# The gated unit's groups on three banks in turn, and a job of 16 columns as four column strips

## The chip, the cores and the metric

The kernel runs on one core of one Trainium2 chip. A core has five engines with queues of their own: TensorE (PE in the profile; its weight loads are listed apart as PEld), VectorE (DVE), ScalarE (ACT), GpSimd (POOL) and SyncE (SP, which here only issues DMAs). They meet through semaphores. TensorE writes into PSUM, which the kernel holds as one tensor `P` of 128 partitions by 8 banks by 512 float32; ScalarE and VectorE read it from there. The metric is the device time of one execution in microseconds (us), the median of several runs.

## What is computed

One step of a decoder block: two branches from one input projection, merged by gates, then a mixture of experts. The part that matters here, cut from the reference:

```python
h = _rmsnorm(x, norm_mix_w)
proj = h @ w_in                       # 1024 -> 4624 columns
qkv, z, a, b, u, gate_a, gate_b = jnp.split(proj, cuts, axis=-1)
...
g = -jnp.exp(a_log) * jax.nn.softplus(a + dt_bias)      # 8 columns "a": the decay of each head
beta = jax.nn.sigmoid(b)                                # 8 columns "b": the gate of each head
o, s_new = _gated_delta(q, k, v, g, beta, s_delta)
...
ys = jax.nn.gelu(ys).astype(x.dtype)                    # branch two, 512 channels
ys = ys * jax.nn.sigmoid(ys @ w_glu)                    # the gated unit
y_b = ys @ w_b_up
```

There are 1024 prompt tokens and 32 sample tokens, 1056 in all, and everything is float32.

## The kernel before

The activations `hT` lie transposed in SBUF: 8 slabs of 128 channels by 1056 tokens. The input projection runs as 32 **jobs** (36 with those that come later), each of which makes 128 columns of `proj` for all tokens: for each of the 8 slabs, three matmuls of 352 tokens (`NBK = 3`, `TBK = 352`), one for each of three PSUM banks. Even jobs write banks 0 to 2, odd jobs banks 3 to 5 (line 688). Job n waits until its weights are in (`s_w`, a ring of three) and until job n-2 has been read out of PSUM (`s_jev`, which counts jobs that were read). A float32 matmul of the program is two pairs of a weight load and a matmul in the trace, so a job of 24 matmuls has 48 records on TensorE.

The order on each engine is the order in which its block is written. Around the change it is this:

- **Jobs 8 to 15** make gate columns. ScalarE reads each out with a sigmoid and stores it to `gate_d`.
- **The gated unit** (lines 846 to 854) comes after job 15: for each of 4 blocks of 128 output channels, three groups over the tokens (408, 408 and 272 columns), each of 4 matmuls that add up in one bank. Every group takes bank 7 through `bank7()`, which waits until the group before has been read. ScalarE reads a group with a sigmoid (line 2140); after each third, VectorE multiplies (lines 1516 and 1518), and ScalarE stores the product to `y2_d` (lines 2144 and 2146). After the fourth it waits until the stores have landed and raises `s_free` (line 2149), since what comes next lies in the same SBUF.
- **Job 16**, called `AB`, has only 16 useful columns, the 8 of `a` and the 8 of `b`. Its weights are loaded by two DMAs to columns 0 to 7 and 32 to 39 of a block of 64 (line 2462), and its matmuls are 64 columns wide. The results are in partitions 0 to 7 and 32 to 39 of three banks. ScalarE reads them with two activations (line 2155): one adds `dt_bias` on the way, the other is the sigmoid of `beta`. Both go into the tile `G0`.
- **The decay chain** follows: VectorE (line 1527) and ScalarE (lines 2162 to 2164) make the softplus with two more tables of functions, VectorE ends it with a running sum (lines 1529 to 1532), and SyncE sends it out (line 2539 on).
- **Job 17 on** make q, k and v. ScalarE reads job 17 (lines 2215 to 2226), VectorE adds up the convolution (lines 1558 to 1566), ScalarE takes silu and squares (lines 2274 and 2275), and TensorE, which is by then three quarters through job 18, waits for the squares and sums them (line 914), before it goes on.

## Time and profile before

| | us |
|---|---|
| Median of 3 runs before (1571.62 to 1573.28) | 1572.18 |
| The profiled execution's own time | 1573.48 |
| Its span on the core | 1571.7 |
| TensorE matmul busy in it (93% of the span) | 1467.8 |
| From the first matmul of the gated unit to the first of job 16 (326.85 to 365.94) | 39.1 |
| From there to the first of job 17 (365.94 to 380.28) | 14.3 |

The times of the views are microseconds from the start of the span, so a row can be put beside another by its start. In a row of the timeline come the start, how long it lasts, the engine (PEld is the weight load), the line, the operation, output and input with shapes and the count of instructions that were merged; in brackets how long the engine had been idle, and what released it. Neighbours of one line are merged, so the busy time of a merged row is from its first start to its last end. A matmul's record is longer than the time to the next one, since matmuls are pipelined.

### The profile page before, as it was taken

Reading aid. Unit: us, or ns where it says so; the run is one execution under the profiler, and the core shown is the slowest. Engines: PE = TensorE matmul, PEld = TensorE weight load, DVE = VectorE, ACT = ScalarE, POOL = GpSimd, SP = SyncE. Lnnn points to the kernel's source line nnn. Section 1 sums busy time; section 2 is a strip of 40 time slices with the busy share of each in tenths; the row PEclk is TensorE's granted clock in tenths of the full one; section 3 lists DMA queues with packets and bytes.
Section 4 is the critical chain, followed back from the end, with each engine's and each line's share of the span. In section 5 each row is a group of like instructions: output and inputs, shape, how many; then the busy total and the mean of one; then the engine's idle time right before and its main releaser. Section 6 shows DMA issues by size and latency. Waiting matters only on the chain.

```text
span 1571.7 us, 20070 instructions
## 1 busy us (share of the span) xinstructions
PE 1467.8 (93%) x8091; PEld 905.8 (58%) x8091; DVE 715.1 (45%) x1315; ACT 347.8 (22%) x589; POOL 151.2 (10%) x160
## 2 busy tenths in 40 slices
PE   7999999989999999999878899999889999999965
PEld 6666666645666556656767566755554444444432
DVE  4668685212324433699677243365533212121116
ACT  4212100112636543232213100111111111111113
POOL 1000010000001000044055000010110000000013
PEclk9998999999999999999989999999989999999998
DMA  5254893432321112325323343532569999999938
GB/s 173 84 95 77 244 289 103 112 121 82 104 77 56 42 42 96 67 79 169 90 76 92 118 150 95 175 124 107 181 248 372 368 366 374 363 372 364 376 120 318
DMA packets 232277, 273.50 MB, mean 174 GB/s; under 512 B 62516, under 2 KB 167336, under 8 KB 231920
## 3 DMA queue, kind: packets, MB, share of 16 engines
q1 hardware_dynamic: 204628, 203.54, 41.6%
q10 hardware_dynamic: 18140, 34.48, 5.8%
q0 software_dynamic: 9408, 34.08, 5.6%
q8 instruction: 69, 1.13, 0.3%
q14 instruction: 32, 0.26, 0.1%
HBM read 188.83 MB, written 83.24 MB: 173 GB/s over the span
## 4 chain that ended last, share of the span: by engine, by line
PE 80%; DVE 8%; issue 5%; POOL 3%; ACT 2%; DMA 2%; ACTq 0%; POOLq 0%; SPq 0%; DVEq 0%
PE P L694 28%; PE P L1239 13%; PE P L1063 7%; PE P L1219 6%; PE P L1150 5%; PE P L851 2%; POOL arena L599 2%; DVE arena L1545 2%; PE P L1186 2%; DVE arena L1547 1%; PE P L1107 1%; PE P L720 1%; PE P L914 1%; PE P L826 1%; PE P L883 1%
## 5 line engine op out<-in xcount | busy, mean ns | idle before, releaser
L694 PE MATMUL P<-arena 128*128 128x352 f32 (+1 forms) x1728 | 535.2, 465 | 4.0 <-ACT arena L2293 2.8
L694 PEld LDWEIGHTS P<-arena 128*128 128x128 f32 (+1 forms) x1728 | 322.2, 190 | 191.4 <-issue 30.5
L1239 PE MATMUL P<-arena 128*128 128x512 f32 x512 | 225.0, 592 | 0.0
L1239 PEld LDWEIGHTS P<-arena 128*128 128x128 f32 x512 | 94.8, 190 | 107.1 <-issue 107.1
L1063 PE MATMUL P<-arena 128*128 128x352 f32 x384 | 117.7, 467 | 4.3 <-DMA arena<-y_d 4.3
L1219 PE MATMUL P<-arena 128*128 128x512 f32 x256 | 115.3, 593 | 0.9 <-DVE arena L1946 0.9
L1906 DVE COPY arena<-P 128x512 f32<-128x512 f32 x32 | 22.1, 692 | 205.2 <-PE P L1186 202.3
L1063 PEld LDWEIGHTS P<-arena 128*128 128x128 f32 x384 | 74.3, 194 | 45.9 <-issue 6.4
L1150 PE MATMUL P<-arena 128*128 128x512 f32 x192 | 87.0, 599 | 0.0
L1219 PEld LDWEIGHTS P<-arena 128*128 128x128 f32 x256 | 46.2, 190 | 47.5 <-issue 46.4
L2427 ACT ACTIVATE arena<-P 128x256 f32<-128x256 f32 x32 | 12.3, 385 | 207.2 <-PE P L1239 207.2
L1914 DVE COPY arena<-P 128x512 f32<-128x512 f32 x32 | 22.1, 692 | 73.6 <-PE P L1219 73.4
L1150 PEld LDWEIGHTS P<-arena 128*128 128x128 f32 x192 | 34.9, 190 | 36.0 <-issue 35.9
L1564 DVE SCALAR_TENSOR_TENSOR arena<-arena,par 128x1024 f32<-128x1024 f32 x36 | 46.3, 1285 | 14.8 <-ACT arena L2226 13.9
L599 POOL TENSOR_TENSOR arena<-arena,N 128x256 f32<-128x256 f32 x48 | 44.8, 933 | 76.6 <-ACT arena L2317 26.1
L2024 ACT ACTIVATE arena<-P 128x1056 f32<-128x1056 f32 x20 | 21.0, 1051 | 133.9 <-PE P L694 133.3
L1711 DVE TENSOR_TENSOR arena<-P,arena 128x352 f32<-128x352 f32 x24 | 12.6, 524 | 77.9 <-PE P L1063 77.9
L645 POOL DMA_DIRECT2D arena<-x_d x31 | 16.5, 533 | 310.7 <-ACT arena L2408 307.9
L1516 DVE TENSOR_TENSOR arena<-arena 128x1024 f32<-128x1024 f32 x4 | 8.1, 2020 | 69.5 <-ACTq L2141 69.5
L2416 ACT ACTIVATE arena<-P 128x512 f32<-128x512 f32 x32 | 19.1, 597 | 92.4 <-PE P L1219 92.4
L851 PE MATMUL P<-arena 128*128 128x408 f32 (+1 forms) x96 | 32.4, 480 | 6.8 <-ACT arena L2140 6.8
L1186 PEld LDWEIGHTS P<-shift_id,arena 128*128 128x128 f32 x248 | 29.0, 141 | 16.4 <-issue 16.4
(411 smaller groups left out, 1763.9 us busy)
## 6 DMA issues: line engine op xcount, KB each, us to landing
arena<-in_w_expert_up_dram SPq DMA_DIRECT2D x32, 2048.0 KB, 13.7
arena<-in_w_expert_down_dram SPq DMA_DIRECT2D x32, 1024.0 KB, 7.8
arena<-in_w_in_dram SPq DMA_DIRECT2D x36, 512.0 KB, 4.1
x_d<-zero SPq DMA_DIRECT2D x4, 4096.0 KB, 20.2
arena<-x_d POOLq DMA_DIRECT2D x32, 512.0 KB, 6.0
y_d<-arena ACTq DMA_DIRECT2D x32, 512.0 KB, 7.9
gate_d<-arena ACTq DMA_DIRECT2D x16, 528.0 KB, 4.2
arena<-gate_d SPq DMA_DIRECT2D x24, 352.0 KB, 3.1
```

What stands on the lines that cost most here:

```text
L599: pool.tensor_tensor(ring[c % 2], src[:, :, c, :], N1[:, q, :, c].unsqueeze(2).broadcast_to([128, HP, C]), ALU.mult).then_inc(s_kb, 1)
L694: m = pe.matmul(P[0:p, b + j, 0:TBK], w[:, k, 0:p], hT[:, k, TBK * j:TBK * j + TBK], start=f, stop=l)
L851: m = pe.matmul(bank[:, 0:sn * KS], wglu[:, k, 128 * j:128 * j + 128], ygT[:, k, s0:s0 + sn, :].rearrange("p a b -> p (a b)"), start=k == ...
L1063: i = pe.matmul(P[:, o, 0:TBK], w[:, k, 128 * m:128 * m + 128], v[:, k, t:t + TBK], start=k == 0, stop=k == 3)
L1150: m = pe.matmul(P[:, b + o, :], MIX[:, k, 128 * i:128 * i + 128], W_O[:, k, 512 * o:512 * o + 512], start=k == 0, stop=k == KD - 1)
L1186: m = pe.transpose(bank[:, k * 128:k * 128 + 128], xg[i % 2][:, (k0 + k) * 128:(k0 + k + 1) * 128], ident)
L1219: m = pe.matmul(P[:, b + o, :], hactT[i % 2][:, k, :], WD[i % NWE][:, k, 512 * o:512 * o + 512], start=k == 0, stop=k == 1)
L1239: m = pe.matmul(P[:, i % 2, :], xgT[i % 2][:, k, :], WU[i % NWE][:, k, :], start=k == 0, stop=k == KD - 1)
L1545: link(dve.tensor_tensor(pv, tv[:, :, :, 0:i], NAb[:, :, i * C:i * C + i].unsqueeze(2).broadcast_to([128, 2, i, i]), ALU.mult))
L1564: link(dve.scalar_tensor_tensor(acc[:, 0:SEQ], raw[:, i:i + SEQ], wcol, acc[:, 0:SEQ], ALU.mult, ALU.add))
L1906: dve.tensor_copy(xgT[i % 2][:, 0:4].rearrange("p a b -> p (a b)"), bk).then_inc(s_xgT6, 1)
L1914: dve.tensor_copy(yo[i % 2][:, 512:1024], P[:, 3 + 2 * (i % 2), :]).then_inc(s_yov, 1)
```

## The change

Two parts. In the gated unit the groups take banks 0, 1, 2 in turn. TensorE waits before the first group until jobs up to 14 have been read and bank 7 is free, and from the fourth group on until the group three places back has been read. The same at the end, ahead of job 16.

Job 16 loads its 16 columns with one DMA, side by side. The 1056 tokens are cut in four strips of 264 (`TSTRIP`). For each slab, four matmuls with the same 16 columns as weights write their strip to partitions 0, 32, 64 and 96 of one bank. So it has 32 matmuls of 16 columns by 264 tokens in the place of 24 of 64 by 352. ScalarE reads it with eight activations in the place of two: four copies of 8 rows to `G0`, and four sigmoids of all 16 rows to a new tile `Gb`, whose rows 8 to 15 are `beta`. The bias is added by a new instruction of VectorE.

```diff
+TSTRIP = NT // 4
...
+        Gb = at(r + 6144, NT)
...
-            return 16 * (n // NWR + 1 + (n >= AB and n % NWR == AB % NWR))
+            return 16 * (n // NWR + 1)
...
-                p = 64 if JOBS[n][0] == "ab" else 128
                 for k in range(KD):
                     f, l = k == 0, k == KD - 1
-                    for j in range(NBK):
-                        m = pe.matmul(P[0:p, b + j, 0:TBK], w[:, k, 0:p], hT[:, k, TBK * j:TBK * j + TBK], start=f, stop=l)
+                    if JOBS[n][0] == "ab":
+                        for j in range(4):
+                            m = pe.matmul(P[32 * j:32 * j + 2 * H, b, 0:TSTRIP], w[:, k, 0:2 * H],
+                                          hT[:, k, TSTRIP * j:TSTRIP * j + TSTRIP], start=f, stop=l)
+                    else:
+                        for j in range(NBK):
+                            m = pe.matmul(P[:, b + j, 0:TBK], w[:, k, :], hT[:, k, TBK * j:TBK * j + TBK], start=f, stop=l)
...
             pe.wait_ge(s_ygT, 16 * 5)
+            pe.wait_ge(s_jev, N_JOBS_S5 - 1)
+            pe.wait_ge(s_7f, n7[0])
             for j in range(4):
                 for q, (s0, sn) in enumerate(((0, 3), (3, 3), (6, 2))):
-                    bank = bank7()
+                    if j > 0:
+                        pe.wait_ge(s_7f, n7[0] - NBK + 1)
+                    n7[0] += 1
+                    bank = P[:, q, :]
...
+            pe.wait_ge(s_7f, n7[0] - NBK + 1)
...
             dve.wait_ge(s_ab2, 1)
+            link(dve.tensor_scalar(G0[0:H], G0[0:H], abp[:, 1:2], None, ALU.add))
             dve.scalar_tensor_tensor(G1[0:H], G0[0:H], -1.0, G0[0:H], ALU.mult, ALU.max).then_inc(s_ab, 1)
...
-                    read7(act.activation(sg[:, s0 * KS:(s0 + sn) * KS], bank7()[:, 0:sn * KS], ACT.Sigmoid))
+                    read7(act.activation(sg[:, s0 * KS:(s0 + sn) * KS], bank7(q)[:, 0:sn * KS], ACT.Sigmoid))
...
-            for p0, func, bias in ((0, ACT.Identity, abp[:, 1:2]), (32, ACT.Sigmoid, 0.0)):
-                ins = act.activation(blocks3(G0[p0:p0 + H, 0:NT]), P[p0:p0 + H, b:b + NBK, 0:TBK], func, bias=bias)
-                if p0 == 0:
+            for j in range(4):
+                link(act.activation(G0[0:H, TSTRIP * j:TSTRIP * j + TSTRIP], P[32 * j:32 * j + H, b, 0:TSTRIP], ACT.Copy))
+            for j in range(4):
+                ins = act.activation(Gb[0:2 * H, TSTRIP * j:TSTRIP * j + TSTRIP], P[32 * j:32 * j + 2 * H, b, 0:TSTRIP],
+                                     ACT.Sigmoid)
+                if j < 3:
                     link(ins)
...
-                    for i in range(2):
-                        c = COL_AB + i * H
-                        sp.dma_start(wring[n % NWR][:, :, 32 * i:32 * i + H], w_view[:, :, c:c + H]).then_inc(s_w[n % NWR], 16)
+                    sp.dma_start(wring[n % NWR][:, :, 0:2 * H], w_view[:, :, COL_AB:COL_AB + 2 * H]).then_inc(s_w[n % NWR], 16)
...
-                    sp.dma_start(beta_d, G0[32:32 + H, 0:SEQ]).then_inc(s_gcd, 16)
+                    sp.dma_start(beta_d, Gb[H:2 * H, 0:SEQ]).then_inc(s_gcd, 16)
```

How the instructions stand, first on TensorE: the start of the gated unit before. `s_7f` counts the groups that have been read, so each group waits for the one before it.

```order
265 L851 MATMUL P<-arena 128x408 [waits s_7f,s_ygT]
266 L851 MATMUL P<-arena 128x408 x3
267 L851 MATMUL P<-arena 128x408 [waits s_7f]
268 L851 MATMUL P<-arena 128x408 x3
269 L851 MATMUL P<-arena 128x272 [waits s_7f]
270 L851 MATMUL P<-arena 128x272 x3
```

The same place of TensorE in the changed kernel, where the waits from the fourth group on are for the group three places back.

```order
265 L862 MATMUL P<-arena 128x408 [waits s_7f,s_jev,s_ygT]
266 L862 MATMUL P<-arena 128x408 x7
267 L862 MATMUL P<-arena 128x272 x4
268 L862 MATMUL P<-arena 128x408 [waits s_7f]
269 L862 MATMUL P<-arena 128x408 x3
```

The matmuls are the same ones in the same order; three groups run before the first wait.

The end of the gated unit and job 16 on TensorE before, up to the wait for the squares (`s_sq`).

```order
287 L851 MATMUL P<-arena 128x272 [waits s_7f]
288 L851 MATMUL P<-arena 128x272 x3
289 L694 MATMUL P<-arena 64x352 [waits s_jev,s_wr1]
290 L694 MATMUL P<-arena 64x352 x23
291 L694 MATMUL P<-arena 128x352 [waits s_jev,s_wr2]
292 L694 MATMUL P<-arena 128x352 x23
293 L694 MATMUL P<-arena 128x352 [waits s_jev,s_wr0]
294 L694 MATMUL P<-arena 128x352 x17
295 L908 MATMUL P<-shift_id,CV 27x128 [waits s_7f,s_conv]
296 L914 MATMUL P<-arena,head_ones 128x352 [waits s_sq]
```

The same place of TensorE in the changed kernel.

```order
284 L862 MATMUL P<-arena 128x272 [waits s_7f]
285 L862 MATMUL P<-arena 128x272 x3
286 L696 MATMUL P<-arena 16x264 [waits s_jev,s_wr1,s_7f]
287 L696 MATMUL P<-arena 16x264 x31
288 L700 MATMUL P<-arena 128x352 [waits s_jev,s_wr2]
289 L700 MATMUL P<-arena 128x352 x23
290 L700 MATMUL P<-arena 128x352 [waits s_jev,s_wr0]
291 L700 MATMUL P<-arena 128x352 x17
292 L918 MATMUL P<-shift_id,CV 27x128 [waits s_7f,s_conv]
293 L924 MATMUL P<-arena,head_ones 128x352 [waits s_sq]
```

Nothing moved past anything; 32 narrow matmuls stand where 24 stood.

ScalarE from the last store of the gated unit on, before (`s_y2a` and `s_y2b` count the stores that have landed).

```order
110 L2146 DMA y_d<-arena 128x1056 [waits s_gluo]
111 L2155 ACTIVATE arena<-P,abp 8x1056 [waits s_y2a,s_y2b,s_job,s_abp]
112 L2155 ACTIVATE arena<-P 8x1056 [waits s_act]
113 L2162 ACT_TABLE_LOAD [waits s_jev]
114 L2162 ACTIVATE arena<-arena 8x1056 [waits s_ab]
```

And in the changed kernel.

```order
110 L2157 DMA y_d<-arena 128x1056 [waits s_gluo]
111 L2166 ACTIVATE arena<-P 8x264 [waits s_y2a,s_y2b,s_job,s_abp]
112 L2166 ACTIVATE arena<-P 8x264 [waits s_act] x3
113 L2168 ACTIVATE arena<-P 16x264 [waits s_act] x4
114 L2176 ACT_TABLE_LOAD [waits s_jev]
115 L2176 ACTIVATE arena<-arena 8x1056 [waits s_ab]
```

Two instructions became eight, each waiting for the one before it; the waits ahead of them are the same. (A tile that the views call `y_d` here is `y2_d`.)

## Rows read from the trace of the kernel before

**Rows 1.** The page: the chain that ended last, by engine.

```profile
PE 80%; DVE 8%; issue 5%; POOL 3%; ACT 2%; DMA 2%; ACTq 0%; POOLq 0%; SPq 0%; DVEq 0%
```

**Rows 2.** The timeline of the gated unit: four groups.

```profile
326.85 2.90 PE L851 MATMUL P<-arena 128*128 128x408 f32 x8
...
329.79 0.51 ACT L2140 ACTIVATE arena<-P 128x408 f32<-128x408 f32 x1 [1.69 <-PE P L851]
...
330.35 3.01 PE L851 MATMUL P<-arena 128*128 128x408 f32 x8 [0.60 <-ACT arena L2140]
330.80 0.19 PEld L851 LDWEIGHTS P<-arena 128*128 128x128 f32 x1 [0.15 <-issue]
331.14 0.19 PEld L851 LDWEIGHTS P<-arena 128*128 128x128 f32 x1 [0.15 <-issue]
...
334.02 2.10 PE L851 MATMUL P<-arena 128*128 128x272 f32 x8 [0.66 <-ACT arena L2140]
...
336.67 3.01 PE L851 MATMUL P<-arena 128*128 128x408 f32 x8 [0.55 <-ACT arena L2140]
```

**Rows 3.** Who waited for whom, 310 to 420: us in total, times, longest.

```profile
PE P L851 <- ACT arena L2140: 6.8, 11, 0.7
```

**Rows 4.** The end of the gated unit and job 16: the timeline, 365 to 381.

```profile
365.94 29.40 PE L694 MATMUL P<-arena 128*64 128x352 f32 x98
...
368.94 0.33 ACTq L2146 DMA_DIRECT2D y_d<-arena  x1
...
371.95 0.91 DVE L1524 MEMSET arena<- 8x1024 f32 x1 [3.04 <-ACTq L2149]
...
380.28 14.79 PEld L694 LDWEIGHTS P<-arena 128*128 128x128 f32 x51 [0.55 <-issue]
380.38 0.37 SPq L2465 DMA_DIRECT2D arena<-in_w_in_dram  x1
380.45 1.13 ACT L2155 ACTIVATE arena<-P,abp 8x1056 f32<-8x1056 f32 x1 [13.95 <-PE P L694]
...
380.79 0.59 SPq L2498 DMA_DIRECT2D y_d<-zero  x1
```

**Rows 5.** The timeline of line 806, two 64-column matmuls side by side: 162.4 to 163.

```profile
162.47 0.19 PEld L806 LDWEIGHTS P<-arena 128*64 128x64 f32 x3 [0.49 <-issue]
162.47 0.34 PE L806 MATMUL P<-arena 128*64 128x136 f32 x2
...
162.47 1.61 PE L806 MATMUL P<-arena 128*64 128x136 f32 x24
```

**Rows 6.** The decay chain, and job 17 read out: the timeline, 382 to 406.

```profile
382.81 1.25 DVE L1527 SCALAR_TENSOR_TENSOR arena<-arena 8x1056 f32<-8x1056 f32 x1 [9.81 <-ACTq L2160]
...
390.67 0.76 DVE L1531 TENSOR_SCALAR arena<-arena,abp 8x1056 f32<-8x1056 f32 x1
391.53 2.28 DVE L1532 TENSOR_TENSOR_SCAN arena<-arena 8x1024 f32<-8x1024 f32 x1
...
394.85 0.76 ACT L2218 ACTIVATE arena<-P 128x704 f32<-128x704 f32 x1 [5.09 <-PE P L694]
...
396.41 0.17 DVE L1558 COPY CV<-arena 128x3 f32<-128x3 f32 x1 [2.61 <-ACT arena L2221]
...
397.96 1.28 DVE L1564 SCALAR_TENSOR_TENSOR arena<-arena,par 128x1024 f32<-128x1024 f32 x1 [1.17 <-ACT arena L2226]
...
403.90 1.08 ACT L2275 ACTIVATE arena<-arena 128x1056 f32<-128x1056 f32 x1
...
405.35 1.94 PE L914 MATMUL P<-arena,head_ones 128*128 128x352 f32 x6
```

**Rows 7.** The page's DMA issues: size of one, and us from issue to landing.

```profile
gate_d<-arena ACTq DMA_DIRECT2D x16, 528.0 KB, 4.2
```

**Rows 8.** Stretches: PE, PEld, DVE, ACT, POOL busy (count); then clock, DMA share, GB/s.

```profile
123.00:133.00 10.00, 10.00 (x36) 8.42 (x36) 5.31 (x14) 0.00 (x0) 0.00 (x0) 0.50 0.48 110
365.90:380.20 14.30, 14.30 (x49) 6.49 (x48) 3.22 (x4) 0.40 (x1) 0.00 (x0) 1.00 0.18 76
```

More of the change, by code:

```diff
@@ L2539, in _ @@
                     sp.dma_start(gc_d, gc_row[0:H, :]).then_inc(s_gcd, 16)
-                    sp.dma_start(beta_d, G0[32:32 + H, 0:SEQ]).then_inc(s_gcd, 16)
-                    for q, rows_ in enumerate((G1[0:H], G0[32:32 + H])):
+                    sp.dma_start(beta_d, Gb[H:2 * H, 0:SEQ]).then_inc(s_gcd, 16)
+                    for q, rows_ in enumerate((G1[0:H], Gb[H:2 * H])):
                         for t in range(TS):
```

## The prediction

> **What bounds the kernel now.** I read the chain that ended last first: 80% of the span lies on TensorE, 8% on VectorE and 2% on ScalarE [rows 1]. Then I took the timeline of the stretch that the change touches. From 326.85 to 380.28 TensorE is the engine that the others wait for: it runs the gated unit to 365.94 and job 16 to 380.28, and ScalarE waits 13.95 us for job 16 [rows 2, 4]. So time taken from TensorE here moves all that follows forward, as long as no chain on ScalarE, VectorE or a store becomes the later one. The sum therefore has three terms: the pauses between the gated unit's groups, the length of job 16, and what the decay chain gives back.
>
> **Term 1, the groups.** A group of 408 columns starts at 326.85, ScalarE begins to read it at 329.79, and the next starts at 330.35 [rows 2]. Within a group the weight loads are 0.34 us apart [rows 2], so its 8 records take 8 x 0.343 = 2.74 us; the stride to the next group is 3.50 and then 3.67 us. The rest, 0.8 to 0.9 us, is the matmul's way out of the array (not yet over when the profile's TensorE is free again; it counts 0.6 of it as idle, 6.8 us in 11 waits [rows 3]) and the 0.5 us of reading. A record costs 0.84 ns per column, so a group of 272 needs 8 x 0.228 = 1.83 us, and its stride now is 336.67 - 334.02 = 2.65. All twelve groups: 8 x 2.74 + 4 x 1.83 = 29.2 us, against 365.94 - 326.85 = 39.1 now. With three banks a group waits for the one three places back, whose reading was over two groups ago: ScalarE needs 0.5 us for a group in every 2.74 [rows 2]. I find no pause left inside. The first wait is for jobs up to 14, and job 15 follows them on TensorE for as long as any full job, 14.57 us (394.85 - 380.28) by job 17 [rows 4, 6], so it is free. After a third group, reading it, the product and the issue of its store are over in 368.94 + 0.33 - 365.94 = 3.3 us [rows 4], and three groups will take 7.3. So 39.1 - 29.2 = 9.9 us, less 0.1 for going over to the narrow form: **9.8 us**. From below I would take 9.3 (0.05 us left at each boundary), from above 10.1.
>
> **Term 2, job 16.** Now 48 records of 352 columns from 365.94 to 380.28, 14.3 us, 0.295 each [rows 4]. The width of the weights (64 of 128 columns) buys nothing: 14.3 us is also what a full job takes, from 380.28 to ScalarE's start at 394.85 being 14.57 [rows 4, 6]. The new job streams the same number of columns in all (32 x 264 = 24 x 352), as 64 records of 0.222 us. One after the other they are 14.2 us, no gain. It gains only if strips that lie in different columns of the array run at the same time. The trace has no strips of 32 columns; the nearest row is line 806 with two of 64. There 24 records of 136 columns are over in 1.61 us [rows 5]; by 0.84 ns per column they would need 24 x 0.114 = 2.74 one after the other, and half of that, 1.37, plus the 0.28 by which the last record outlasts its stream, is 1.65. So two run at once. How they do it decides what four do. The program gives each matmul as two records, both on the same strip, and each must wait for the other. If the order of the program were kept strictly, the second half of one strip would overlap only the first half of the next, never more than two at once, and four strips would gain no more than two. But in line 806 two matmuls have started when only the third weight load begins [rows 5], 0.06 us after the first: the second strip has begun ahead of the first strip's second half. So I read a strip as a stream of its own. Then each of the four has 16 records x 0.222 = 3.55 us, and with 0.2 for coming and going the job takes 3.75: 14.35 - 3.75 = **10.6 us**. The bounds are 14.4 (no overlap, gain 0) and 3.75; I take the lower one, since the row nearest in kind shows full overlap.
>
> The Trainium skill bears on this in "TensorE: Matmul & The Clock Gate", Part 3. It says that matmuls start and end strictly in program order, which speaks against the change: by that rule at most two records overlap here, job 16 takes about 7.3 us and the sum below would be 3 us smaller. The same part gives a measured gain of 3.07 for four tiles in rows of the array; as an estimate by that figure job 16 would take 14.2 / 3.07 = 4.6 us. The first record of line 806 disagrees with the rule; no row here shows four strips.
>
> **Term 3, what comes behind job 16.** Count from T, the first record of job 16 (365.94 now). The last group is read and multiplied, the store goes out at T + 3.0 and VectorE sees `s_free` at T + 6.0 [rows 4]. ScalarE reads job 16 only after that store has landed. This was hidden by the 14.3 us of job 16, and is no longer: job 16 ends at T + 3.75, ScalarE starts at T + 6.05. It then has 8 activations in the place of two. One of 264 columns is bounded by the 0.40 of a 272-column sigmoid and the 0.51 of one with 408 [rows 2]; with the wait between them 0.43 each, 3.4 us, against 382.81 - 380.45 = 2.36 now, its signal included [rows 4, 6]. They end at T + 9.45. VectorE's new bias instruction is like the 0.76 us of line 1531 [rows 6], 0.85 with its wait, and has no cover. From VectorE's start at line 1527 (382.81) to the end of the running sum (391.53 + 2.28 = 393.81) the chain takes 11.0 us [rows 6]. So VectorE is free at T + 9.45 + 0.15 + 0.85 + 11.0 = T + 21.45, and ScalarE, by the same shift, at T + 17.4.
>
> Job 17 ends for ScalarE at T + 3.75 + 14.57 = T + 18.3, so ScalarE is in time by 0.9 us where it now waits 5.09 [rows 6]. VectorE is wanted for the convolution's first product 397.96 - 394.85 = 3.11 after ScalarE's start, and 0.45 earlier for two copies: at T + 20.95. It comes at T + 21.45, 0.5 late. Behind it the squares end at 403.90 + 1.08 = 404.98, and TensorE wants them at 405.35 [rows 6]: 0.3 of slack once the signal is paid. The stall at line 914 is 0.2 us if the store lands as now.
>
> It may land later, because SyncE now sends weights (and clears a part of `y_d`) as soon as job 16 is over, at T + 3.85 instead of T + 14.4 [rows 4], 0.85 us behind the store. A store of the same size that shares the DMA engines has a median of 4.2 us [rows 7], this one some 2.6 to 3. I take 0.3 more: **0.5 us** given back. Bounds: 0 and 2.0. Job 18 reuses banks 0 to 2 and needs job 16 read by T + 18; that is over at T + 9.5. The edits with one answer: one DMA for the weights in place of two, issued well ahead of use, costs nothing; `beta` from `Gb` has the same rows and size; SyncE waits for the decay chain until 3 us after job 17, not 1 before, and holds back the weights of job 20, which are wanted two jobs later.
>
> **The sum.** 9.8 + 10.6 - 0.5 = 19.9 us. The profiled execution took 1573.48 us (span 1571.7), so it would become 1553.6; it lies 1.3 above the median of 1572.18, and against that median the forecast is **1552.3 us**. What follows is bound by the same chain through jobs 17 to 31, so it moves as a whole.
>
> **The rivals.**
> - *Two at a time* (14%). Job 16 takes 7.3 us, the decay chain starts 1.45 later but job 17 3.5 later, and no stall is left: 9.8 + 7.1 = 16.9 us, 1555.3. For it: the program's order puts both halves of a strip together. Against it: rows 5.
> - *The store becomes the bound* (8%). Weights and clearing delay it by up to 2.5 us, and all of it comes through, since the slack is spent: the stall is 2.7, gain 17.7, 1554.5. For it: the 4.2 of the gate stores [rows 7]. Against it: this store is issued first.
> - *One half does nothing* (4%). The strips take turns (14.4 us), gain 9.8; or the groups keep their stride because the array is drained between banks, gain 10.1. Either way about 1562.
> - *The clock falls: slower* (2%). Around 123 us, with small matmuls that leave the array little to do, the granted clock is 0.50, full speed being 2.4 GHz [rows 8]; 1.00 in job 16 now. If strips with 16 of 128 columns count as little work and also take turns, 64 records x 0.44 = 28.4 us, 14.1 more, and if 4 us of job 17 run at 1.2 GHz too, 2.0 more are lost: 16.1 - 9.8 = 6.3 slower, 1578.6. It needs job 16 above 24.1 us to lose anything, and both faults at once.
>
> **How the numbers follow.** The forecast case has 70%, 2% is left for what I don't see; about 0.2%, 3.1 us, is what a measurement of this kernel can tell from no change. The range takes in the first three cases: from 1550.4 (no stall, both terms at their best, and the few us at half clock that lie elsewhere falling well) to 1556.6 (two at a time, with 1.3 for the spread). Faster has the first four cases and half of the rest, 97%; I give 95%, since all the terms but one are sure only if nothing later is fixed in time. Within 0.2% 2%, slower 3%.
>
> **What would show it.** Right: the twelve groups start 2.74 and 1.83 us apart with no wait for ScalarE between them; job 16's 64 records are over in under 4 us, four starting together; ScalarE's idle time ahead of job 16 ends with the landing of the store, not with TensorE; its wait ahead of job 17 has shrunk from 5.1 to about 1; and a first pause of a few tenths stands at line 914 in job 18. Wrong: job 16 near 7 us (two at a time) or 14 (turns); a pause of 2 to 3 us at line 914 (the store); a clock below 1.00 between the unit and job 18; or the time after job 18 not moved by the same amount as its start.

## The result, and the profile after

| | us |
|---|---|
| Changed kernel, median of 4 runs (1548.94 to 1551.89) | 1551.03 |
| Kernel before beside it, median of 4 runs (1571.14 to 1573.28) | 1571.9 |
| Ratio, with its 95% interval | 0.986 (0.9846 to 0.9874) |
| Profiled execution of the changed kernel, and its span | 1551.32, 1549.6 |

The change makes the kernel faster by 1.4%. The medians are 20.9 us apart; against the 1572.18 of before the ratio gives 22.0 us, and its interval 19.8 to 24.2. The sum of the prediction was 19.9. So the direction and the size came out, but 1572.18 less 22.0 is 1550.2, just below the low end of the forecast range, 1550.4. The interval leaves 0 to 4 us more than the sum, and the first question is whether these come from the stretch that was changed. Here are its landmarks in the two profiled executions, by TensorE's first matmul of each piece.

| | before | after | gained | predicted |
|---|---|---|---|---|
| gated unit, to job 16 | 39.09 | 29.35 | 9.74 | 9.8 |
| job 16, to job 17 | 14.34 | 3.69 | 10.65 | 10.6 |
| job 17, to the sum of squares in job 18 (line 914, now 924) | 25.06 | 25.59 | -0.53 | -0.5 |
| these three together | 78.50 | 58.63 | 19.87 | 19.9 |
| start of the span to the gated unit | 326.85 | 324.62 | 2.2 | 0 |
| line 914 (924) to the end | 1166.40 | 1166.34 | 0.1 | 0 |

The three terms are within 0.06 us. The rest, 2.2 us, lies ahead of everything that the change touches.

First the page: busy time, share of the span and count of TensorE, and the chain that ended last by engine. TensorE has lost 14.9 us of busy time, from 1467.8, and still holds the chain as in [rows 1].

```profile
PE 1452.9 (94%) x8107; PEld 898.5 (58%) x8107; DVE 717.7 (46%) x1316; ACT 348.6 (22%) x595; POOL 152.4 (10%) x160
...
PE 79%; DVE 8%; issue 5%; ACT 3%; POOL 3%; DMA 2%; ACTq 0%; POOLq 0%; DVEq 0%; SPq 0%
```

The gated unit after, in the timeline (start, length, engine, line, operation, tiles; in brackets the idle time and what ended it). The first fence is TensorE alone, the second ScalarE alone.

```profile
324.62 9.88 PE L862 MATMUL P<-arena 128*128 128x408 f32 x31
```

```profile
327.56 0.51 ACT L2151 ACTIVATE arena<-P 128x408 f32<-128x408 f32 x1 [1.69 <-PE P L862]
330.36 0.51 ACT L2151 ACTIVATE arena<-P 128x408 f32<-128x408 f32 x1 [2.29 <-PE P L862]
332.19 0.40 ACT L2151 ACTIVATE arena<-P 128x272 f32<-128x272 f32 x1 [1.32 <-PE P L862]
334.87 0.51 ACT L2151 ACTIVATE arena<-P 128x408 f32<-128x408 f32 x1 [2.28 <-PE P L862]
337.67 0.51 ACT L2151 ACTIVATE arena<-P 128x408 f32<-128x408 f32 x1 [2.29 <-PE P L862]
```

In [rows 2] each row of TensorE ended with a wait for ScalarE; now TensorE's records run together without one (31 in the window of this view, and all 96 of the unit in the trace), and it is ScalarE that waits, some 2.3 us for each wide group. The read of a narrow group (272 columns) starts 1.83 us after the one before it, that of a wide group 2.68 to 2.80, against the 2.74 and 1.83 that the first term used. The waits of [rows 3] have no row left between line 862 and ScalarE.

Job 16 and what follows it, in the timeline of all engines, with the rows that answer to [rows 4] and [rows 6]:

```profile
353.96 3.25 PEld L696 LDWEIGHTS P<-arena 128*16 128x16 f32 x64 [0.36 <-issue]
353.96 3.76 PE L696 MATMUL P<-arena 128*16 128x264 f32 x64
...
357.11 0.33 ACTq L2157 DMA_DIRECT2D y_d<-arena  x1
...
357.65 25.12 PE L700 MATMUL P<-arena 128*128 128x352 f32 x84
...
358.20 0.80 SPq L2510 DMA_DIRECT2D y_d<-zero  x1
360.50 1.62 ACT L2166 ACTIVATE arena<-P 8x264 f32<-8x264 f32 x4 [5.97 <-DMA y_d<-arena]
...
362.16 1.62 ACT L2168 ACTIVATE arena<-P 16x264 f32<-16x264 f32 x4
...
372.22 0.76 ACT L2232 ACTIVATE arena<-P 128x704 f32<-128x704 f32 x1 [0.55 <-PE P L700]
...
373.44 2.28 DVE L1543 TENSOR_TENSOR_SCAN arena<-arena 8x1024 f32<-8x1024 f32 x1
...
375.75 0.17 DVE L1569 COPY CV<-arena 128x3 f32<-128x3 f32 x1
...
382.11 1.08 ACT L2289 ACTIVATE arena<-arena 128x1056 f32<-128x1056 f32 x1
...
383.25 2.04 PE L924 MATMUL P<-arena,head_ones 128*128 128x352 f32 x6 [0.36 <-ACT arena L2289]
```

Job 16's 64 records are over in 3.76 us (3.69 from its first record to job 17's), where 48 took 14.3. ScalarE's idle time ahead of it no longer ends with TensorE (13.95 us in [rows 4]) but with the landing of the store that was issued at 357.11. VectorE goes from the running sum to the copies of the convolution with no idle time between, where it had waited 2.61 us [rows 6], so the chain is now the later one there. And line 924 waits: 0.36 us are put down to ScalarE, and the stretch from job 17's first matmul is 0.53 us longer than before.

The same stretch in three pieces (busy time and count of PE, PEld, DVE, ACT, POOL; then TensorE's granted clock, the share of the DMA engines and GB/s). The clock stays at 1.00, that is 2.4 GHz, in all of it:

```profile
324.60:353.90 29.30, 29.30 (x97) 18.05 (x95) 6.70 (x6) 6.33 (x12) 0.00 (x0) 1.00 0.33 110
353.90:357.60 3.70, 3.70 (x65) 1.77 (x64) 2.38 (x2) 0.40 (x1) 0.00 (x0) 1.00 0.35 146
357.60:383.20 25.60, 25.28 (x89) 15.98 (x85) 12.37 (x16) 16.22 (x25) 0.00 (x0) 1.00 0.31 86
```

### The profile page after: what moved, and what is told of

It is laid out like the page before. It is cut to its first block, busy times and chain, and to the rows that moved or that the text cites. A ratio compares the mean times of both kernels' runs of the same rounds, so it can differ in the third digit from the quotient of the medians.

```text
span 1549.6 us, 20108 instructions
## 1 busy us (share of the span) xinstructions
PE 1452.9 (94%) x8107; PEld 898.5 (58%) x8107; DVE 717.7 (46%) x1316; ACT 348.6 (22%) x595; POOL 152.4 (10%) x160
## 4 chain that ended last, share of the span: by engine, by line
PE 79%; DVE 8%; issue 5%; ACT 3%; POOL 3%; DMA 2%; ACTq 0%; POOLq 0%; DVEq 0%; SPq 0%
PE P L700 27%; PE P L1249 13%; PE P L1073 7%; PE P L1229 6%; PE P L1160 5%; PE P L862 2%; PE P L1196 2%; POOL arena L601 2%; PE P L1117 1%; DVE arena L1556 1%; PE P L832 1%; PE P L893 1%; PE P L884 1%; PE P L1097 1%; PE P L924 1%
## 5 line engine op out<-in xcount | busy, mean ns | idle before, releaser
L700 PE MATMUL P<-arena 128*128 128x352 f32 x1680 | 520.7, 465 | 4.0 <-ACT arena L2307 2.8
L700 PEld LDWEIGHTS P<-arena 128*128 128x128 f32 x1680 | 315.5, 191 | 183.8 <-issue 22.7
L1249 PEld LDWEIGHTS P<-arena 128*128 128x128 f32 x512 | 94.8, 190 | 107.3 <-issue 107.3
L1073 PE MATMUL P<-arena 128*128 128x352 f32 x384 | 116.8, 464 | 2.6 <-DMA arena<-y_d 2.6
L1073 PEld LDWEIGHTS P<-arena 128*128 128x128 f32 x384 | 73.8, 192 | 43.9 <-issue 3.9
L1229 PEld LDWEIGHTS P<-arena 128*128 128x128 f32 x256 | 46.2, 190 | 47.5 <-issue 46.4
L1160 PEld LDWEIGHTS P<-arena 128*128 128x128 f32 x192 | 34.9, 190 | 36.0 <-issue 35.9
L1556 DVE TENSOR_TENSOR arena<-arena 128x2 f32<-128x2 f32 (+30 forms) x31 | 33.9, 1093 | 1.1
```

What stands on the lines that cost most here:

```text
L700: m = pe.matmul(P[:, b + j, 0:TBK], w[:, k, :], hT[:, k, TBK * j:TBK * j + TBK], start=f, stop=l)
L1073: i = pe.matmul(P[:, o, 0:TBK], w[:, k, 128 * m:128 * m + 128], v[:, k, t:t + TBK], start=k == 0, stop=k == 3)
L1160: m = pe.matmul(P[:, b + o, :], MIX[:, k, 128 * i:128 * i + 128], W_O[:, k, 512 * o:512 * o + 512], start=k == 0, stop=k == KD - 1)
L1229: m = pe.matmul(P[:, b + o, :], hactT[i % 2][:, k, :], WD[i % NWE][:, k, 512 * o:512 * o + 512], start=k == 0, stop=k == 1)
L1249: m = pe.matmul(P[:, i % 2, :], xgT[i % 2][:, k, :], WU[i % NWE][:, k, :], start=k == 0, stop=k == KD - 1)
L1556: link(dve.tensor_tensor(pv, tv[:, :, :, 0:i], NAb[:, :, i * C:i * C + i].unsqueeze(2).broadcast_to([128, 2, i, i]), ALU.mult))
```

## The experiments

Theory: three terms, independent of each other as far as TensorE goes; the strips run at once because each is a stream of its own; the decay chain now sets line 914 and passes on any further delay one for one; the rest of the difference to the measured time is not the change's. The rivals, term by term, are that the parts need each other, that the narrow weights and not the strips make job 16 short, that records leave strictly in program order, and that the stall comes from something other than the chain. All kernels here compute the whole result. In "stretch" I give the time from the first matmul of the gated unit to line 914 (924), before 78.50, after 58.63.

### The changed kernel again

> The changed kernel as it is, once more. The trace of it puts the time from the gated unit's first matmul to the sums of line 914 (now 924) 19.9 us below before, as the three terms said, and 2.2 us more were gained ahead of the gated unit, where nothing was changed. Theory A: those 2.2 us and the difference between the forecast 19.9 and the measured 20.9 come from where the stretches at the half clock fall; then the difference of medians lies between 19 and 21.5 us, and the executions with a lower mean granted clock are the longer ones, about 1.7 us for each 3.4 us at half clock. Theory B: the change itself gives 1 to 2 us more than the three terms, somewhere behind the stretch; then the difference is 21 to 22 us again whatever the clock.

Nothing is edited. Median 1551.48 (5 runs, 1548.56 to 1556.48) against 1572.33 (11 runs), 20.85 us apart, ratio 0.9867 (0.9848 to 0.9887). Stretch 58.64. The difference is inside theory A's 19 to 21.5 and below theory B's 21 to 22, but only by 0.15, which the interval doesn't resolve.

> The changed kernel once more, beside the next two on one chip. So far its executions went from 1548.6 to 1556.5 and before's from 1570.0 to 1575.1, while the traces of all kernels have the same stretch lengths to 0.01 us but for the clock. If the 1 us by which the measured gain (20.9) exceeded the stretch's own (19.9) is where the half-clock stretches fell by chance, this set moves toward 19.9 from before: median difference 19 to 21.5.

Again no edit, on another chip. Median 1552.21 (4 runs, 1549.94 to 1554.13) against 1572.61 (9 runs), 20.4 us apart, ratio 0.9864 (0.9843 to 0.9884). Stretch 58.63.

The stretch repeats to 0.01 us, while single executions of one kernel lie up to 8 us apart. All 13 executions of the changed kernel have a mean of 1551.6 (standard deviation 2.3), all 24 runs of the kernel before in the three timings 1572.6 (1.7): 21.0 us apart, with an interval of about 1.5 either way (twice the square root of 2.3²/13 + 1.7²/24). The 19.9 of the trace is inside it.

### One part alone

```diff
+            pe.wait_ge(s_jev, N_JOBS_S5 - 1)
+            pe.wait_ge(s_7f, n7[0])
...
-                    bank = bank7()
+                    if j > 0:
+                        pe.wait_ge(s_7f, n7[0] - NBK + 1)
+                    n7[0] += 1
+                    bank = P[:, q, :]
...
+            pe.wait_ge(s_7f, n7[0])
...
-                    read7(act.activation(sg[:, s0 * KS:(s0 + sn) * KS], bank7()[:, 0:sn * KS], ACT.Sigmoid))
+                    read7(act.activation(sg[:, s0 * KS:(s0 + sn) * KS], bank7(q)[:, 0:sn * KS], ACT.Sigmoid))
```

This is the kernel before with the three banks. Ahead of job 16, which stays as it was and needs all three of them, TensorE waits for the last group too.

> The three banks alone; job 16 stays as before, and since it writes all three banks it waits until the last group has been read (0.7 us that the full change doesn't pay). Theory A, the terms as forecast: 9.8 - 0.7 = 9.1 us faster, 1562.8. The stride of the groups 2.74 and 1.83 us. No stall at line 914, since job 16 still covers the store. Theory B (more from one part): over 10.5 us faster.

Gated unit 29.96, job 16 14.34, job 17 to line 914 25.06; the stretch is 69.37, a gain of 9.13. Timed: 1563.63 (5 runs) beside 1572.33, ratio 0.9942 (0.9928 to 0.9955). The 0.6 us over the changed kernel's 29.35 is the wait for the last group, which the changed kernel avoids since job 16 uses one bank only. TensorE's timeline shows it as idle time ended by ScalarE:

```profile
356.87 13.53 PE L694 MATMUL P<-arena 128*64 128x352 f32 x45 [0.55 <-ACT arena L2145]
```

The other half is the changed kernel with `bank7()` for every group, as before:

```diff
-            pe.wait_ge(s_jev, N_JOBS_S5 - 1)
-            pe.wait_ge(s_7f, n7[0])
...
-                    if j > 0:
-                        pe.wait_ge(s_7f, n7[0] - NBK + 1)
-                    n7[0] += 1
-                    bank = P[:, q, :]
+                    bank = bank7()
...
-            pe.wait_ge(s_7f, n7[0] - NBK + 1)
...
-                    read7(act.activation(sg[:, s0 * KS:(s0 + sn) * KS], bank7(q)[:, 0:sn * KS], ACT.Sigmoid))
+                    read7(act.activation(sg[:, s0 * KS:(s0 + sn) * KS], bank7()[:, 0:sn * KS], ACT.Sigmoid))
```

> The four strips alone; the gated unit stays on bank 7 with its pauses. Theory A: job 16 takes 3.7 us in the place of 14.3, and the decay chain comes 0.5 late at line 914, as in the full change: 10.1 us faster, 1561.8. Theory B: over 11.5 us faster. If the decay chain were no cost, 10.6 and no pause at line 914 beyond 0.1.

Gated unit 39.09, job 16 3.70, job 17 to its line 919 25.56; stretch 68.35, a gain of 10.15. Timed: 1560.3 (6 runs) beside the same 1572.33, ratio 0.993 (0.9914 to 0.9946). These medians are 12.0 us apart, which is in theory B's range; the interval, 8.5 to 13.5 us, holds both theories, and it is the trace that speaks for the first. The pause of 0.5 us comes with the strips alone:

```profile
392.91 2.04 PE L919 MATMUL P<-arena,head_ones 128*128 128x352 f32 x6 [0.34 <-ACT arena L2284]
```

9.13 + 10.15 = 19.28, and with the 0.6 us that the banks alone can't have, 19.9. Neither part needs the other for more than that.

### Why job 16 is short

Three kernels vary what the strips do. The first keeps the 16-column weights and gives up the strips:

```diff
-                        for j in range(4):
-                            m = pe.matmul(P[32 * j:32 * j + 2 * H, b, 0:TSTRIP], w[:, k, 0:2 * H],
-                                          hT[:, k, TSTRIP * j:TSTRIP * j + TSTRIP], start=f, stop=l)
+                        for j in range(NBK):
+                            m = pe.matmul(P[0:2 * H, b + j, 0:TBK], w[:, k, 0:2 * H],
+                                          hT[:, k, TBK * j:TBK * j + TBK], start=f, stop=l)
```

> Job 16 with weights of 16 columns, but no strips: 24 matmuls of 352 tokens to partitions 0 to 15 of three banks, read by two activations; the gated unit on three banks, with a wait for its last group. If narrow weights alone cost and save nothing, job 16 takes 48 x 0.295 + 0.2 = 14.4 us as before. If part of the gain came from the width, less than 12.

The second has two strips in the place of four, in the same 32 matmuls, at partitions 0 and 64 of two banks:

```diff
-                            m = pe.matmul(P[32 * j:32 * j + 2 * H, b, 0:TSTRIP], w[:, k, 0:2 * H],
+                            m = pe.matmul(P[64 * (j % 2):64 * (j % 2) + 2 * H, b + j // 2, 0:TSTRIP], w[:, k, 0:2 * H],
```

In both of these kernels ScalarE's reads follow the results to where they now lie (not shown). Job 16 writes more than one bank again, so TensorE waits for the gated unit's last group ahead of it, as with the banks alone.

> The four pieces of 264 tokens in two column strips (partitions 0 and 64, banks 0 and 1), 32 matmuls. Strips as streams of their own: each strip has 32 records x 0.223 = 7.1 us, job 16 takes 7.3, and records start in pairs 0.22 apart. If what counts is only how many matmuls are in flight, whatever their strip: 3.7 us as with four strips. Line 914 without a pause, since job 17 ends 3.6 us later.

The third keeps four strips and exchanges the loops, so that all 16 records of a strip stand together (the branch goes ahead of the loop over slabs):

```diff
+                if JOBS[n][0] == "ab":
+                    for j in range(4):
+                        for k in range(KD):
+                            m = pe.matmul(P[32 * j:32 * j + 2 * H, b, 0:TSTRIP], w[:, k, 0:2 * H],
+                                          hT[:, k, TSTRIP * j:TSTRIP * j + TSTRIP], start=k == 0, stop=k == KD - 1)
+                    m.then_inc(s_job, 1)
+                    return
```

> Four strips, but the program has all 8 slabs of a strip before the next strip's: 16 records in a row on one strip. If each strip takes its records as soon as they are in TensorE's queue, however deep they stand, job 16 is 3.7 to 5 us as before. If records can only start a few places ahead of their turn, the strips follow one another with little overlap: 11 to 14.4 us. The estimate between: overlap for some 10 to 30 instructions gives 6 to 10.

From job 16's first matmul to job 17's: 14.30, 7.23 and 11.72 us; one execution each took 1559.82, 1557.35 and 1560.38 beside 1572.5. None of the three has a stall at line 924 (25.06 from job 17 on, as before the change), the two strips included, as expected for them. TensorE's timelines, first of 16 columns without strips, then of two strips, then of strip after strip:

```profile
354.55 14.37 PE L696 MATMUL P<-arena 128*16 128x352 f32 x48 [0.55 <-ACT arena L2151]
```

```profile
356.86 7.30 PE L696 MATMUL P<-arena 128*16 128x264 f32 x64 [0.55 <-ACT arena L2151]
```

```profile
356.79 11.79 PE L695 MATMUL P<-arena 128*16 128x264 f32 x64
```

Narrow weights alone buy 0.04 us. Two strips run at twice the speed and four, in the changed kernel, at nearly four times. In the third kernel, with four strips free, 11.7 us is far above 3.7, and still below the 14.2 of one after the other. Its records say why. Each of the 64 lasts 0.386 us as in the changed kernel, but the pace changes (PE and PEld of line 695 alone; a record still running from the stretch before is counted too):

```profile
356.70:359.40 2.70, 2.61 (x12) 1.18 (x13) 1.00 0.42 174
359.40:360.30 0.90, 0.90 (x10) 0.44 (x8) 1.00 0.20 80
```

Twelve records stand alone, 0.22 us apart. Then the second strip begins, at 359.48, when the first has its last four to run, and these four run beside the second strip's first four. The trace does not name a record's strip; that a strip runs one record at a time is read from these twelve, which by the program's order are all the first strip's. I read the whole as: records leave in the order of the program, and a strip that is busy takes some more behind the one it runs; the engine goes no further in the program until the last of these has a place. Two forms of it were open, that at most three records are passed over in all, or that each strip holds three behind the running one. They part when the program gives each strip four records in a row, two slabs of two halves:

```diff
+                if JOBS[n][0] == "ab":
+                    for kk in range(0, KD, 2):
+                        for j in range(4):
+                            for k in (kk, kk + 1):
+                                m = pe.matmul(P[32 * j:32 * j + 2 * H, b, 0:TSTRIP], w[:, k, 0:2 * H],
+                                              hT[:, k, TSTRIP * j:TSTRIP * j + TSTRIP], start=k == 0, stop=k == KD - 1)
+                    m.then_inc(s_job, 1)
+                    return
```

> Four strips, two slabs of a strip in a row: 4 records on strip 0, then 4 on strip 1, and so on. The rule that the orders so far fit: a record starts as soon as its strip is free and no more than three records ahead of it in the program's order have not yet started. Played through for the orders run so far it gives 3.68 us with one slab per turn (measured 3.69), 11.71 with all eight (measured 11.72), 7.25 with two strips (measured 7.23). Here it gives 4.35 us for job 16. If the limit were two records, 5.9; four, 4.1; one, 7.7; and if the eight-slab order was slow for another reason, 3.7.

Job 16 took 3.72 us (one execution: 1557.13 beside 1569.45), as short as with two in a row, where three in all had been put at 4.35. That form falls. By the other form each strip takes four, one running and three behind it, so a run of four per strip never blocks; the first row here is the first 0.9 us, with the 16 records of all four strips:

```profile
358.00:358.90 0.90, 0.85 (x16) 0.52 (x17) 1.00 0.00 0
358.90:359.80 0.90, 0.90 (x23) 0.52 (x16) 1.00 0.30 122
```

If each strip holds three, a run of eight has to block: the first strip is alone until its fifth record starts and its last three are held, 4 x 0.22 = 0.89 us later. The last kernel once more, with four slabs in the place of two:

```diff
-                    for kk in range(0, KD, 2):
+                    for kk in range(0, KD, 4):
                         for j in range(4):
-                            for k in (kk, kk + 1):
+                            for k in range(kk, kk + 4):
```

> Four strips, four slabs of a strip in a row (8 records). The rule of three records passed in all has fallen (3.72 measured with two slabs per turn, 4.35 expected). In its place: records leave in the program's order, each into a queue of its own strip, which holds three besides the running one; a full queue holds up all that stands behind. Played through it gives 3.69 (measured 3.69), 3.69 (3.72), 11.72 (11.72) and 7.26 (7.23, two strips). Here it gives 8.15 us for job 16; a queue of two 9.7, of four 6.6, of six 4.4; no such limit 3.7.

Measured 8.23 (one execution: 1558.38 beside 1569.77), against 8.15 by three per strip and 9.7 and 6.6 by two and four. Four records in the first 0.9 us, and from then on two strips at a time (9 and 10 with those that were running):

```profile
353.70:354.60 0.90, 0.85 (x4) 0.40 (x5) 1.00 0.00 0
354.60:355.50 0.90, 0.90 (x9) 0.44 (x8) 1.00 0.29 122
355.50:356.40 0.90, 0.90 (x10) 0.44 (x8) 1.00 1.04 432
```

The one rule gives 3.7, 3.7, 8.15, 11.7 and 7.3 for runs of 2, 4, 8 and 16 and for two strips; measured were 3.69, 3.72, 8.23, 11.72 and 7.23. The rule was formed after the run of 16 and corrected after the run of 4; only the run of 8 is a forecast that it passed. Whether the limit counts records, weight loads or columns is not shown: in all these kernels a record has 264 columns and a weight load of its own.

### The chain behind job 16

Theory: the stall at line 914 is the decay chain's lateness, so 1.7 us more on the chain give 1.7 us more of stall. The four copies are made twice:

```diff
-            for j in range(4):
+            for j in (0, 1, 2, 3, 0, 1, 2, 3):
                 link(act.activation(G0[0:H, TSTRIP * j:TSTRIP * j + TSTRIP], P[32 * j:32 * j + H, b, 0:TSTRIP], ACT.Copy))
```

> The changed kernel with the four copies of job 16 made twice (12 activations in the place of 8), which puts the decay chain 1.65 us later and touches nothing else. If the chain's lateness comes through at line 914 in full, the pause there goes from 0.5 to 2.2 us. If it has slack, it stays near 0.5.

Job 17 to line 924 took 27.25, a stall of 2.19; stretch 60.29, one execution 1556.68. The timeline shows the wait for ScalarE grown from 0.36 to 1.94:

```profile
385.02 2.04 PE L924 MATMUL P<-arena,head_ones 128*128 128x352 f32 x6 [1.94 <-ACT arena L2289]
```

The kernel with two slabs in a row gives the same answer with a small step the other way: there the store landed sooner, ScalarE began 6.27 us after job 16's first record and not 6.54, and the stall was 0.24 and not 0.53.

The other way, the chain is shortened. ScalarE adds the bias itself, so VectorE's new instruction goes:

```diff
-            link(dve.tensor_scalar(G0[0:H], G0[0:H], abp[:, 1:2], None, ALU.add))
...
-                link(act.activation(G0[0:H, ...], P[32 * j:32 * j + H, b, 0:TSTRIP], ACT.Copy))
+                link(act.activation(G0[0:H, ...], P[32 * j:32 * j + H, b, 0:TSTRIP], ACT.Identity,
+                                    bias=abp[:, 1:2]))
```

> The changed kernel with only the bias back on ScalarE: the four copies to G0 become four activations with the bias, and VectorE's added instruction goes. That takes 0.85 us out of the decay chain, 0.3 more than its lateness. The pause at line 914 goes from 0.53 to about 0, and the stretch becomes 58.1 us as with the early chain. By time within 1.5 us of the changed kernel, 0.5 better if the clock falls even out.

Stretch 58.22: the stall is 0.13 (25.18 from job 17 on) and not 0.53. Of the 0.8 us that VectorE saves, 0.4 are spent on ScalarE, whose four reads take 2.0 us with the bias and 1.62 without. The next kernel has the bias on ScalarE too; besides, ScalarE reads job 16 before it waits for the store and tells VectorE right after the four reads, and VectorE's first instruction of the chain stands ahead of its wait for `s_free` (these last two edits, of the bias and of VectorE, are not shown):

```diff
-            act.wait_ge(s_y2[0], 32)
-            act.wait_ge(s_y2[1], 32)
-            act.sem_inc(s_free, 3)
...
+            act.sem_inc(s_ab2, 1)
             for j in range(4):
                 ins = act.activation(Gb[0:2 * H, ...
...
-            act.sem_inc(s_ab2, 1)
+            act.wait_ge(s_y2[0], 32)
+            act.wait_ge(s_y2[1], 32)
+            act.sem_inc(s_free, 3)
```

> The full change with the decay chain moved forward: the bias is added by ScalarE's copies again (no instruction of VectorE for it), ScalarE reads job 16 before it waits for the stores of the gated unit, and VectorE is told after the four copies, not after the sigmoids. If the decay chain is what holds up line 914: ScalarE reads job 16 some 3.9 us after its first matmul (6.5 in the changed kernel), VectorE is free 2 to 3 us before it is wanted for job 17, the pause at line 914 goes from 0.5 us to 0.1 or less, and the kernel is 0.5 us faster than the changed one, 1550.5. If the pause has another cause (the load on ScalarE behind job 17), it stays at 0.5.

> The early decay chain once more: its trace has the stretch 0.53 us shorter than the changed kernel's, yet its four executions lay 3 us above it. If that was chance (its trace shows 6.8 us at half clock near 445 us, the changed kernel's none), it now comes within 1.5 us of the changed kernel, on either side. If the earlier chain itself brings on clock falls behind it, it stays 2 to 4 us slower.

The same kernel was run twice: stretches 58.10 and 58.09, no stall, 25.06 from job 17 to line 924 as before the change. The timeline of the first of them has ScalarE waiting for TensorE, not for the DMA, and 3.54 us of slack ahead of job 17:

```profile
357.70 2.00 ACT L2161 ACTIVATE arena<-P,abp 8x264 f32<-8x264 f32 x4 [3.32 <-PE P L696]
...
372.06 0.76 ACT L2231 ACTIVATE arena<-P 128x704 f32<-128x704 f32 x1 [3.54 <-PE P L700]
...
382.56 1.94 PE L924 MATMUL P<-arena,head_ones 128*128 128x352 f32 x6
```

Timed, it doesn't beat the changed kernel: 1554.81 (4 runs, where 1550.5 was expected) beside 1551.48 of the changed one, then 1552.01 (4 runs) beside 1552.21; with the bias on ScalarE alone 1552.49 (5 runs) beside the same 1552.21. Half a microsecond in the trace is below what these timings resolve. The first pair stands 3.3 us the other way and the second doesn't repeat that, so it is put down to the spread between executions and not to the earlier chain. So the stall is settled as a mechanism, and its removal is not shown as a gain.

### Where the rest of the time varies

Outside the stretch the executions of one kernel differ. Here are four windows ahead of it; the granted clock is the third number from the end of a row. Before the change, at 122.9 (10.2 us at half clock); after, at 124.0 (6.8 us of it); and the changed kernel again, where a second piece at 159.4 follows its own 10.2 us:

```profile
122.90:133.10 10.20, 10.20 (x37) 8.52 (x37) 5.51 (x14) 0.00 (x0) 0.00 (x0) 0.50 0.49 108
```

```profile
124.00:131.00 7.00, 7.00 (x21) 5.19 (x21) 4.11 (x8) 0.00 (x0) 0.00 (x0) 0.51 0.17 67
```

```profile
121.90:132.10 10.20, 10.20 (x41) 9.20 (x41) 4.85 (x14) 0.00 (x0) 0.00 (x0) 0.50 0.51 112
159.40:162.80 3.40, 3.40 (x25) 2.94 (x26) 0.58 (x1) 0.43 (x1) 0.00 (x0) 0.50 1.13 340
```

The gated unit begins at 326.85, 324.62 and 328.83 in these three. Over all 15 traces its start follows the time at 1.2 GHz ahead of it with a correlation of 0.97 and 0.56 us for each us, from 324.4 with 6.8 us of it to 328.8 with 13.7. So the 2.2 us which the trace of after has gained ahead of the change are of this kind, and the same kernel loses them again in its next traced execution.

Behind line 914 there is a second such place, some 62 us on. These are two executions of the same changed kernel, the first result's and the third timing's:

```profile
440.00:450.00 10.00, 7.28 (x69) 4.79 (x64) 0.69 (x1) 5.62 (x7) 0.00 (x0) 1.00 0.01 2
```

```profile
448.20:455.00 6.80, 6.10 (x11) 3.61 (x12) 0.00 (x0) 4.28 (x5) 0.00 (x0) 0.50 0.01 2
```

TensorE is partly idle there (7.28 of 10 us busy), and in 11 of the 15 traces the clock falls in this place. The time from line 914 to the end runs from 1164.2 to 1170.8 over the 15 traces, and follows its time at half clock only loosely (correlation 0.56). What else moves it by several us I have not found.

The timed executions bear out the first part of the expectation of the first repeat: those with a lower mean granted clock are the longer ones, with a correlation of -0.78 over the 13 of the changed kernel and -0.90 over the 20 of the kernel before in the two repeats. The size comes to about 1.2 us for each 3.4 us at half clock, where 1.7 was expected; the clocks are known to three digits only, which flattens such a slope.

## Why the prediction's terms were right, and its range too narrow

Point by point, by its own steps.

- **Term 1.** 29.35 against 29.2 + 0.1 for going over to the narrow form. The strides of 2.74 and 1.83 came out, no pause was left, and the first wait was free. With the banks alone it was the same, but for the wait ahead of job 16.
- **Term 2.** 3.69 against 3.75. The decision between two at a time and four was taken on [rows 5], and was right. In the trace four records start within 0.03 us (353.96 to 353.98) and the next four 0.22 us behind them; since the program gives each strip two records in a row, three of the first four have passed an earlier strip's second half. What holds is order within a strip, and a limit on how far ahead the engine goes. The rule of the Trainium skill that the prediction quotes, that matmuls start and end strictly in program order ("TensorE: Matmul & The Clock Gate", Part 3), doesn't hold between column strips here: by it job 16 would have taken about 7.3 us, and it took 3.69. The prediction's reading, that a strip is a stream of its own, was too strong: it is that only while the program changes the strip at least every fourth record. With this change's order of loops both readings give 3.7, and only the exchanged loops (11.72) and the run of eight (8.23) tell them apart. The Trainium skill's other figure in that part, 3.07 for four tiles in rows of the array, is too small for these four strips in its columns, which have 14.34 / 3.69 = 3.9.
- **Term 3.** 0.53 against 0.5, but two of its parts were off and cancelled in part. From job 16's first record (353.96) the store was issued at 3.15 (forecast 3.0) and ScalarE began at 6.54 (forecast 6.05, and 0.3 for a late store), 0.2 late in all; its eight reads took 3.24 us and not 3.4. VectorE was free at 373.44 + 2.28 - 353.96 = 21.76, where 21.45 and the 0.3 make 21.75. ScalarE had 0.55 us to spare ahead of job 17, against 0.9 less 0.3. The doubled copies show that the slack is gone: 1.66 more on the chain gave 1.66 more of stall. The store does set when ScalarE begins (its wait ends with the landing), but it is 0.2 us late and not the up to 2.5 of the rival *the store becomes the bound*.
- **Nothing later was fixed in time.** In the trace what follows line 914 took 1166.34 and before 1166.40. That they agree so well is luck in part, since this time ranges over 6.7 us in the 15 traces.
- **The sum.** 19.87 in the trace, 19.9 forecast. This part stands.
- **What failed is the term for the spread**, and with it the lower end of the range, in "How the numbers follow". 1550.4 was made from no stall (0.5), both terms at their best, and "the few us at half clock that lie elsewhere falling well", for which only about 1 us was left; the upper end had 1.3 for the spread. Both are too small, and neither was worked out from a row. The three runs of before, 1.7 us apart, had suggested so little. Of the 13 executions of the changed kernel 4 lie below 1550.4 (1548.56 to 1549.94) and none above 1556.6, and 22.0, the gain by the ratio, puts the time at 1550.2. With the gain of 20.9 by the medians it would be 1551.3 and inside the range, so the miss of 0.2 us is itself no larger than the noise. The half clock ahead of the gated unit is worth up to 4.4 us by itself over the 15 traces (324.4 to 328.8), and it falls out differently for one and the same kernel. [rows 8] show ten us of it; how much that varies, one trace couldn't show, and the prediction put about 1 us on it all the same. A term of plus or minus 2 us, on both sides, is what the standard deviation of 2.3 us asks for.

Open: whether the mean gain is really above 19.9. It is 21.0 with 1.5 either way, so it needn't be; and what moves the time behind line 914 from one execution to the next.

## What to carry to other kernels

A matmul with few output columns cost here by its streamed columns and not by its width (14.30 us with 16 columns, 14.34 with 64); cut the stream in four, give each quarter a column strip of 32, and write the loops so that the strip changes with every matmul or every second one (3.69 and 3.72 us), not with every accumulation (11.72). The pauses between groups were cheap to price from the trace: the stride from group to group less what the records' own spacing needs is what banks in turn save, 39.1 less 29.2 us here, and 29.35 was measured. When a long job that hid a chain is cut, add the chain up from its first wait: here 10.65 us of TensorE time gave back only 0.53, and since 1.66 us more on the chain gave 1.66 more of stall, the next microsecond cut there should be lost in full (not run) unless the reads of job 16 go ahead of the store's wait. And give a range the spread of single executions, taken from more than one trace, before its ends are set.

## What the runs showed of the hardware

- The same 64 records took 3.69, 3.72, 8.23 and 11.72 us with 2, 4, 8 and 16 of a strip in a row (each float32 matmul has two). These and the two strips' 7.23 fit one rule, of which the 8.23 alone was forecast: a column strip holds three records behind the one it runs and, once full, holds up all that follow in the program.
- Weights of 16 columns in the place of 64 changed nothing in the job's time (14.30 against 14.34 us), though a weight load's record is 0.096 us long there and 0.19 for 128 columns.
- Four strips of 264 columns ran at 3.9 times the speed of one stream, over 64 records, with the clock at 1.00 throughout.
- Executions of one kernel differ by up to 8 us of 1552, while the changed stretch is the same to 0.01 in the three traces of it. Part of the difference is time at 1.2 GHz (clock 0.50): ahead of the gated unit 6.8 to 13.7 us of it, worth 0.56 us of time for each us. Behind line 914, where the time ranges over 6.7 us, the cause is open.
